# Recurrent layer: order of gates, convolution and output-gate tiles, taps summed in PSUM, recurrence in two halves, three output tiles side by side

## The reference

```python
def rglru_mixer(h, w_in, conv_w, conv_b, w_a, b_a, w_i, b_i, lam, w_out):
    gate, u = jnp.split(h @ w_in, 2, axis=-1)
    u = causal_depthwise_conv(u, conv_w) + conv_b            # four taps
    ub = u.reshape(bsz, seq, LRU_BLOCKS, LRU_BW)             # 4 blocks of 256
    r = jax.nn.sigmoid(jnp.einsum("bsnc,ncd->bsnd", ub, w_a) + b_a)
    i = jax.nn.sigmoid(jnp.einsum("bsnc,ncd->bsnd", ub, w_i) + b_i)
    log_a = -RG_C * r * jax.nn.softplus(-lam)
    a = jnp.exp(log_a)
    b = jnp.sqrt(-jnp.expm1(2.0 * log_a)) * (i * u)
    _, hs = lax.associative_scan(_lru_combine, (a, b), axis=1)   # h_t = a_t h_(t-1) + b_t
    y = jax.nn.gelu(gate) * hs
    return y @ w_out
```

## Time and profile before

| | |
|---|---|
| time, median of 3 runs | 2921.04 us (2920.51 to 2929.26) |
| profiled execution, its own time | 2932.0 us |
| its span in the trace | 2930.2 us |
| mean granted TensorE clock | 0.967 of full |
| TensorE matmul busy | 2762.4 us, 94% |
| VectorE busy | 1078.1 us, 37% |
| ScalarE busy | 1085.9 us, 37% |
| GpSimd busy | 1345.6 us, 46% |
| chain that ended last, TensorE's share | 86% |

### The profile page before, as it was taken

One profiled execution on the slowest core, in us unless ns is written; L12 is line 12 of the kernel. 1 busy time (PEld: TensorE's weight loads), 2 busy tenths in 40 slices (PEclk: granted clock), 3 DMA queues, 4 the chain that ended last, 5 costly groups with the idle time before them and its releaser, 6 DMA issues.

```text
span 2930.2 us, 37914 instructions
## 1 busy us (share of the span) xinstructions
PE 2762.4 (94%) x13516; PEld 2252.8 (77%) x13516; DVE 1078.1 (37%) x1941; ACT 1085.9 (37%) x1766; POOL 1345.6 (46%) x715
## 2 busy tenths in 40 slices
PE   7999999999999999999998999999978689999998
PEld 5756888888757888878767888888866588788886
DVE  5674322113563222023447234221074573432212
ACT  5665332223663322232243333332226343332221
POOL 4555444444384444444445544444433364344442
PEclk9999999999999999999889999999999799999998
DMA  4301323333202233323213312223312231223331
GB/s 156 122 2 39 97 95 100 100 108 97 86 1 83 93 100 100 101 79 102 71 37 101 108 58 86 92 95 105 104 51 79 80 125 62 65 94 100 100 101 64
DMA packets 69089, 251.77 MB, mean 86 GB/s; under 512 B 7672, under 2 KB 7928, under 8 KB 68736
## 3 DMA queue, kind: packets, MB, share of 16 engines
q1 hardware_dynamic: 67104, 244.35, 25.9%
q10 hardware_dynamic: 1888, 6.14, 0.6%
HBM read 248.36 MB, written 2.10 MB: 85 GB/s over the span
## 4 chain that ended last, share of the span: by engine, by line
PE 86%; DVE 9%; issue 2%; ACT 2%; POOL 1%; DMA 0%; DVEq 0%; POOLq 0%; ACTq 0%
PE ps L548 26%; PE ps L550 25%; PE ps L549 25%; PE ps L686 4%; PE ps L711 2%; PE ps L697 2%; DVE acc L1373 1%; DVE xl L1380 1%; POOL pr L514 1%; DVE u_r L1839 1%; DVE u_r L1837 1%; DVE tmpb L1862 0%; DVE pr L1473 0%; DVE y_mid L1683 0%; PE ps L656 0%
## 5 line engine op out<-in xcount | busy, mean ns | idle before, releaser
L467 POOL TENSOR_TENSOR w_lo<-w_raw,w_hi 128x1024 fp32r<-128x1024 f32 x462 | 1115.2, 2418 | 1382.5 <-ACT w_hi L980 1367.4
L548 PE MATMUL ps<-xh,w_hi 128*128 128x512 f32 x2384 | 940.0, 394 | 50.4 <-DVE xl L1380 21.6
L549 PE MATMUL ps<-xl,w_hi 128*128 128x512 f32 x2384 | 933.3, 391 | 0.0
L550 PE MATMUL ps<-xh,w_lo 128*128 128x512 f32 x2384 | 933.0, 391 | 0.0
L980 ACT ACTIVATE w_hi<-w_raw 128x1024 fp32r<-128x1024 f32 x462 | 484.5, 1053 | 531.0 <-PE ps L550 530.3
L548 PEld LDWEIGHTS ps<-xh,w_hi 128*128 128x128 f32 x2384 | 451.5, 189 | 150.3 <-issue 52.5
L549 PEld LDWEIGHTS ps<-xl,w_hi 128*128 128x128 f32 x2384 | 451.5, 189 | 94.3 <-issue 1.7
L550 PEld LDWEIGHTS ps<-xh,w_lo 128*128 128x128 f32 x2384 | 450.8, 189 | 94.9
L548 PE MATMUL ps<-hh,w_hi 128*128 128x512 f32 x704 | 273.9, 389 | 0.0
L550 PE MATMUL ps<-hh,w_lo 128*128 128x512 f32 x704 | 273.9, 389 | 0.0
L549 PE MATMUL ps<-hl,w_hi 128*128 128x512 f32 x704 | 273.9, 389 | 0.0
(11 more groups left out here) (258 smaller groups left out, 2910.4 us busy)
## 6 DMA issues: line engine op xcount, KB each, us to landing
w_raw<-weights_in SPq DMA_DIRECT2D x462, 512.0 KB, 3.4
x<-x_in ACTq DMA_DIRECT2D x4, 512.0 KB, 10.4
mem<-mem_in ACTq DMA_DIRECT2D x2, 1024.0 KB, 4.9
x_out<-x SPq DMA_DIRECT2D x4, 512.0 KB, 2.6
rope<-rope_in ACTq DMA_DIRECT2D x1, 512.0 KB, 11.8
tab<-tables_in ACTq DMA_DIRECT2D x2, 256.0 KB, 2.9
tab<-tables_in ACTq DMA_DIRECT2D x1, 384.0 KB, 12.4
small<-small_in ACTq DMA_DIRECT2D x1, 326.5 KB, 5.1
```

Of the source, the lines that this page charges most:

```text
L467: nc.gpsimd.tensor_tensor(w_lo[:, slot], w_raw[:, slot], w_hi.bitcast(f32)[:, slot], ALU.subtract).then_inc(lo_ready, 1)
L548: nc.tensor.matmul(dst, w_hi[:, slot, w], hi, start=first, stop=False)
L549: nc.tensor.matmul(dst, w_hi[:, slot, w], lo, start=False, stop=False)
L550: return nc.tensor.matmul(dst, w_lo[:, slot, w], hi, start=False, stop=last)
```

## The change

It does five things. (1) After four tiles of c_u, TensorE's order is the list `REC`: the convolution's tiles 4 to 7 (u), the chunks of the recurrence's gates (l) and the output-gate tiles (g) in turns; the stream of weights is laid out in that order. (2) The taps are summed in PSUM's banks 4 to 6 in place of SBUF; ScalarE copies the sum from there twice, to `u_r` and to `u_h`. (3) Each bank of an l chunk has its own wait (`lru_ps`) and its own release (`lru_sig`), and ScalarE's decays, roots and sigmoids are done in two halves of four tiles. (4) On ScalarE the splits of three chunks stand ahead of the first copy. On VectorE the scans stand ahead of the gate's product, apart from it. (5) The first three tiles of c_out are computed side by side, and `sum_squares` moves behind them.

```diff
-    ("c_u", 8, 1), ("lru", 4, 1), ("c_gate", 8, 1), ("c_out", 8, 1), ...
+    ("c_u", 4, 1), ("rec", 16, 1), ("c_out", 8, 1), ...
...
+REC = [("u", 4), ("u", 5), ("l", 0), ("u", 6), ("l", 1), ("u", 7), ("g", 0), ("g", 1), ("l", 2), ("g", 2),
+       ("l", 3), ("g", 3), ("g", 4), ("g", 5), ("g", 6), ("g", 7)]
...
-TOGETHER = {"ab_in": 3, "gu2": 3, "c_u": 3, "gu3": 3}
+TOGETHER = {"ab_in": 3, "gu2": 3, "c_u": 3, "gu3": 3, "c_out": 3}
...
-            for n in range(4):
-                pe.wait_ge(proj_ready, projs.n + 2 * n + 2)
-                c = CHUNK0["lru"] + n
+            for kind, m in REC:
+                c, g = REC_CHUNK[kind, m], REC_BANK[kind, m]
                 pe.wait_ge(lo_ready, c + 1)
-                for m in range(4):
-                    g = BANK0["lru"] + 4 * n + m
-                    pe.wait_ge(evac_done, g - 3)
+                if kind != "l":
+                    rec_bank_free(g)
+                    for k in range(KT):
+                        last = product(ps[:, g % 4, :], c % RING, k, *x_tiles(m, k), k == 0, k == KT - 1)
+                    last.then_inc(chunk_done, 1)
+                    continue
+                pe.wait_ge(proj_ready, projs.n + 2 * m + 2)
+                for q in range(4):
+                    rec_bank_free(g + q)
                     for k in range(2):
...
+                    if q < 3:
+                        last.then_inc(lru_ps, 1)
                 last.then_inc(chunk_done, 1)
             projs.n += 8
-            linear("c_gate", KT, x_tiles)
             linear("c_out", KT, lambda m, k: (y_h[:, k, :], y_l[:, k, :]),
                    ready=lambda k: pe.wait_ge(feat_ready, 4 + k + 1),
-                   after_first=lambda: sum_squares(MEM))
+                   in_fourth={0: lambda: sum_squares(MEM)})
...
-            for m, g in steps("c_u"):
+            for m in range(1, 4):
+                high(CHUNK0["c_u"] + m + LEAD)
+
+            def copy_conv(m):
                 act.wait_ge(u_conv, m + 1)
-                A(u_h[:, m], u_r[:, m], ACT.Copy).then_inc(u_hi, 1)
...
+                A(u_r[:, m], ps[:, 4 + m % 3, :], ACT.Copy)
+                A(u_h[:, m], ps[:, 4 + m % 3, :], ACT.Copy).then_inc(u_hi, 1)
...
+            behind = {
+                ("u", 4): lambda: copy_conv(0), ("u", 5): lambda: copy_conv(1),
+                ("l", 0): lambda: (copy_conv(2), copy_conv(3), sigmoids(0)),
+                ("l", 1): lambda: (copy_conv(4), sigmoids(1)),
+                ("u", 7): lambda: (copy_conv(5), copy_conv(6), decays(0)),
+                ("g", 0): lambda: (copy_conv(7), decay_roots(0)),
+                ("l", 2): lambda: sigmoids(2), ("l", 3): lambda: sigmoids(3),
+                ("g", 3): lambda: decays(4), ("g", 4): lambda: decay_roots(4),
+                ("g", 5): lambda: gelus(0, 5), ("g", 6): lambda: (gelus(5, 6), states_high(0, 2)),
+                ("g", 7): lambda: (gelus(6, 7), states_high(2, 4), gelus(7, 8), states_high(4, 8))}
+            for what in REC:
+                high(REC_CHUNK[what] + LEAD)
+                if what in behind:
+                    behind[what]()
...
+            def conv(m):
+                z, u = z_u[:, m % 2], ps[:, 4 + m % 3, :]
...
+                link(V.tensor_scalar(u, z[:, 3:3 + T], w(3), col("cbias", m), ALU.mult, ALU.add))
...
+            for m in range(8):
+                conv_in(m)
+                if m:
+                    conv_low(m - 1)
+                conv(m)
+                if m == 5:
+                    inputs(0)
+                if m == 6:
+                    inputs(1)
+            conv_low(7)
...
+            taken(("g", 0), gate_r[:, 0])
+            scan(0)
+            taken(("g", 1), gate_r[:, 1])
+            scan(1)
+            scan(2)
+            inputs(2)
+            taken(("g", 2), gate_r[:, 2])
+            scan(3)
+            inputs(3)
...
+            taken(("g", 3), gate_r[:, 3])
+            taken(("g", 4), gate_r[:, 4])
+            scan(4)
+            scan(5)
+            taken(("g", 5), gate_r[:, 5])
...
+            state(0)
+            state(1)
+            scan(6)
+            scan(7)
+            taken(("g", 6), gate_r[:, 6])
+            state(2)
+            state(3)
+            state_low(0)
+            state_low(1)
+            taken(("g", 7), gate_r[:, 7])
```

More of the change, by code:

```diff
@@ L53 @@
     _c += _m * _q
[L55 removed]
+    _g += {"rec": 28, "cmp": 0}.get(_name, _m)
 N_CHUNKS = _c
@@ new lines, in decays, with decay_roots @@
+            def decays(k0):
+                act.wait_ge(lru_sig, 2 * k0 + 8)
+                for k in range(k0, k0 + 4):
+                    A(decay[:, k], r_l[:, k], ACT.Exp, scale=c8[:, k:k + 1])
+                for k in range(k0, k0 + 4):
+                    last = A(r_l[:, k], r_l[:, k], ACT.Tanh, scale=c4[:, k:k + 1])
+                last.then_inc(act_self, 1)
+            def decay_roots(k0):
+                act.wait_ge(act_self, k0 // 4 + 1)
+                for k in range(k0, k0 + 4):
+                    A(r_l[:, k], r_l[:, k], ACT.Sqrt).then_inc(lru_act, 1)
@@ L1870, in _, with state_low @@
-            for m, bank in tiles("c_gate"):
-                scaled(gate_r[:, m], bank).then_inc(evac_done, 1)
-                for k in STATES.get(m, ()):
-                    state(k)
-            state_low(KT - 1)
+                V.tensor_tensor(r_l[:, k], r_l[:, k], gate_r[:, k], ALU.mult).then_inc(feat_in, 1)
+            def state_low(k):
+                dve.wait_ge(feat_hi, 4 + k + 1)
+                V.tensor_tensor(y_l[:, k], r_l[:, k], fp(y_h)[:, k], ALU.subtract).then_inc(feat_ready, 1)
@@ L1875, in _ @@
+            taken(("g", 6), gate_r[:, 6])
[4 more added lines that the diff above has]
+            taken(("g", 7), gate_r[:, 7])
+            dve.wait_ge(dve_self, n_.dself.n)
+            state(4)
+            state_low(2)
+            state(5)
+            state_low(3)
+            state(6)
+            state_low(4)
+            state(7)
+            for k in range(5, KT):
+                state_low(k)
             publish_memory(1)
@@ L1980, in _stream @@
             c_in = v["c_w_in_2"][0]
-            parts += [_chunks(c_in[:, 1024:]), lru(), _chunks(c_in[:, :1024]),
+            pieces = {"u": _chunks(c_in[:, 1024:]), "l": lru(), "g": _chunks(c_in[:, :1024])}
+            parts += [pieces["u"][:4], np.stack([pieces[kind][m] for kind, m in REC]),
                       _chunks(v["c_w_out_2"][0])]
```

121 lines of the change are left out of this document (63 added, 58 removed).

## The result

| | before | change |
|---|---|---|
| time, median | 2923.2 us (2920.5 to 2929.3, 4 runs) | 2901.7 us (2900.2 to 2904.0, 4 runs) |
| ratio | | 0.9921, 95% interval 0.9905 to 0.9936 |
| profiled execution / its span | 2932.0 / 2930.2 us | 2900.9 / 2899.1 us |
| start of the layer (first row-sum product) | 2151.01 | 2147.66 |
| first product of the memory projection | 2350.16 | 2319.23 |

The change is faster by 0.8%: 19 to 28 us by the interval. The layer alone gained 27.6 us, which is 14% of it.

What follows compares the result with a forecast made beforehand. TensorE's waits and low clock in the recurrent layer bound the kernel; 139.2 work, 23.1 waits, 6.0 low clock and 0.7 restarts give 169.0 us, 29 less, so 2921.0 becomes 2892 us, range 2882 to 2904.

Steps and rivals of the forecast that it cites:

- slower handovers: Rival: each start behind another engine costs 0.3 us, not 0.03, or taps 1.2 us; gain 14 to 22; chance 0.12.
- The account: Layer before, 199.2 us: 139.2 of work on 25 tiles, 46.4 of TensorE waits, 13.6 of low clock and restarts.
- Splits ahead of the copies: At u4, which waited 5.12 us before: u4, u5 and l0's first two quarters run with no wait.
- Taps in PSUM: Convolution on VectorE: first tap 0.69 us (bounds 0.55 and 2.28), the other taps 0.75, not slowed by GpSimd.
- the release doesn't happen: Rival in the convolution: the first tap still waits for GpSimd; the walk ends only 1 us later, gain 28 us.
- The waits one by one: TensorE's gaps from l0 to c_out's chunk 3 in the changed layer, nine waits summing to 23.1 us.
- The states: VectorE from g4's end to c_out: 22.0 us with three GpSimd meetings; c_out starts at 2272.0, 5.9 us after g7.
- c_out side by side: c_out's first three tiles take 16.3 us and cover the memory's sum of squares, removing its 7.9 us wait.
- The low clock: TensorE behind waits: five over 2 us at 1.2 us each, 6.0, plus nine restarts at 0.08, 0.7 us.
- Table loads: ScalarE's sigmoids: 1.28 us per load taken; rival of 2.6 us per switch, gain 22 us, chance 0.06.
- Low clock for good: Rival: clock stays at 1.2 GHz through the layer up to g7; layer 17 us later than before, 2938; chance 0.03.
- Fewer meetings: Rival: chunks' low parts fall between VectorE's scans, without GpSimd meetings; walk ends 10 us earlier, gain 39; chance 0.07.

Runs made afterwards that it cites:

- the reordered version: The change with ScalarE's and VectorE's work in the layer put in another order, TensorE's order unchanged: layer 144.29 and 144.43 us, medians 2870.7 and 2873.7 us.
- the second execution: The change run once more, unaltered: layer 172.07 us, median 2903.2 us, ratio to before 0.9911.

## Why the prediction was right, point by point

The direction, the place and, in the layer, nearly the size held: 29 us forecast, 27.6 measured. The launch did less well: 2892 us forecast in a range of 2882 to 2904, 2901.7 measured. Its gain of 21.5 us lies under the 24 to 34 of the forecast and in the 14 to 22 of the rival "slower handovers", though no handover is slower (below). That it fell inside the range is luck in part: 6 us of its distance from the forecast lie outside the layer, in a part that moves by up to 13 us from one profile to the next, and the end of the range was 2 us away.

- **The account** (139.2 of work, 46.4 of waits, 13.6 of low clock) held. The 139.2 is confirmed by the reordered version, whose clock is full: with 4.7 us of waits its layer lasts 144.4. The last term is a remainder; read off the trace of the change, as what up to 24 matmuls behind each wait take over 0.227 us each, 9.6 of the 10.7 are found.
- **Splits ahead of the copies.** u4, u5 and l0's first half ran with no wait, as forecast. It is worth next to nothing all the same: undone, it costs 0.5 us.
- **Taps in PSUM.** 0.69 was taken for the first tap and 0.81 measured, eight times alike; 0.75 for the others and 0.756 measured. Neither meets GpSimd. Worth 7.8 us in the change and 6.9 alone. The prediction's price for the case that the release doesn't happen, 1 us, was far too low: with the taps in SBUF not one tap alone but taps of each of the first three tiles are stretched by GpSimd, and the layer is 7.8 us longer.
- **The waits one by one**, forecast and trace: l0's third quarter 4.2 and 3.78, its fourth 2.2 and 3.05, l1's fourth 4.0 and 3.72, g1 0.9 and none, l2's sigmoids 0.6 and 0.60, l3 2.8 and 2.86, c_out's start 5.9 and 4.92, the sum of squares 0 and 0.46, c_out's chunk 3 1.9 + 0.6 and 2.28. Sum 23.1 and 21.7. The cause given for l1 was the right one: with that pair of copies and the next one early the wait is gone and the layer 6.5 us shorter.
- **The states.** c_out was to start at 2272.0; it starts at 2267.76 + 3.35 = 2271.1. The three meetings with GpSimd are there, each a VectorE operation that starts under a low part and ends behind it:

```profile
2249.75 2.83 DVE L1920 SCALAR_TENSOR_TENSOR tmpb<-decay,r_l 128x512 f32<-128x512 f32 x1
...
2255.07 2.85 DVE L1928 TENSOR_TENSOR r_l<-r_l,gate_r 128x512 f32<-128x512 f32 x2
...
2260.43 2.82 DVE L1920 SCALAR_TENSOR_TENSOR tmpb<-decay,r_l 128x512 f32<-128x512 f32 x1
```

- **c_out side by side.** The sum of squares was to be covered and was, but for 0.46 us and, in the second execution, 1.67; taken strictly, the prediction's own sign of being wrong, "if the sum of squares is waited for", came. Without the part the wait is 8.43. The part is worth 7.7 us. (The prediction has the squares ready at 2288.9; its own 2278.6 + 10.1 is 2288.7.)
- **The low clock was sized too small.** This is the term that failed: 5 x 1.2 + 0.7 = 6.7 us forecast, 10.7 in the trace. The sum of 169.0 thus came out at 171.6, though the waits were 1.4 shorter. A restart of 1.2 us, six matmuls at 0.43, was taken for a wait of over 2 us. At l1's wait it is 1.7: ten matmuls start in the 4.0 us from 2194.10, 2.3 at full speed. Behind c_out's start it is 2.6: 21 matmuls start in the 7.4 us from 2267.76, 4.8 at full speed. Behind the other waits it is 1.6 (l0's fourth quarter), 1.4 (l3), 1.7 (c_out's chunk 3, forecast as 1.9 and 0.6 in two places and charged nothing for the clock) and 0.1 behind l0's third quarter, where one of 1.2 was charged. The five sum to 9.0. A better single number would not have been enough: in the second execution of the change it is 3.0 behind l0's fourth quarter, 2.7 behind l1's wait, 1.7 at l3, 1.4 behind c_out's start and 0.1 behind chunk 3. (The counts in the windows below take in matmuls that began before the window.)

```profile
2194.00:2198.00 4.00, 3.90 (x10) 3.07 (x11) 0.04 (x1) 1.31 (x2) 0.00 (x0) 0.57 0.01 4
2267.00:2271.00 4.00, 3.24 (x8) 2.59 (x9) 4.00 (x8) 2.25 (x5) 0.00 (x0) 0.50 0.02 4
2271.00:2275.00 4.00, 4.00 (x15) 3.16 (x14) 3.83 (x7) 1.55 (x3) 0.00 (x0) 0.74 0.26 39
```

- **From the layer to the launch.** The median came out 9.7 us above the forecast. 1.4 of that is the layer (29 against 27.6), 2.2 the start of the sum (the median of before is 2923.2 beside the change, not 2921.0), and 6.1 that the launches differ by 21.5 us where the layers differ by 27.6. This last part lies outside the layer: the part ahead of it ends up to 13 us earlier or later with the same program. It goes with the granted clock between 1200 and 1500 us: 0.96 in the profile that starts the layer first (2138.5), 0.93 in the five that start it last (2150.0 to 2151.3), 0.94 or 0.95 in the eight between. Why the clock differs there stays open. It is also why the two launches' ratio can't tell 24 from 28 us.
- **Table loads.** The rival had 2.6 us for each. Eight loads stand in the layer in place of five, each of 1.28 us. At l0 the load starts at 2173.32 and takes 1.28 us, and the sigmoids start at 2174.61, 0.01 behind it, as in the earlier trace rows; the copy ahead of the load ends 0.03 before it. The Trainium skill, ScalarE: Activation LUTs, section What ACT_TABLE_LOAD costs, has 1.38 us of drain on top of the same 1.28; no drain shows here, on either side of the load, and the measurement decides.
- **The other rivals.** Slower handovers: none; TensorE starts 0.05 to 0.06 us behind the end of VectorE's operation at all four waits of the l chunks. Low clock for good: no, the windows have 0.90 and more. Nothing moves: no, the layer is 27.6 us shorter. Fewer meetings: no, the three are there.
